# Two token parts under one weight load: a 512-column matmul in the last 64 key tiles, with GpSimd splits and one-hots in fours of tokens

## The chip, the cores and the metric

The kernel runs on one core of one Trainium2 chip. The metric is the device time of one execution in microseconds (us), lower is better. TensorE is written PE (its weight loads PEld), VectorE DVE, ScalarE ACT, GpSimd POOL, and SyncE SP.

## The reference

One residual block over 256 tokens of width 1024, in float32:

```
h = x + W_out( sig(g_conv) * ConformerConv(xn) + sig(g_attn) * DilatedAttn(xn) ),  xn = RMSNorm(x)
y = h + PEER(RMSNorm(h))

def peer(xn, w_q, sub_keys, u_tab, v_tab):          # 16384 experts of one neuron each
    q = (xn @ w_q)  ->  8 heads, 2 halves of 128
    s = q . sub_keys                                  # 128 scores per half
    top 16 of each half, top 16 of the 256 sums       -> 16 experts e and softmax gates per head
    h = einsum('thkd,td->thk', u_tab[e], xn)
    act = gelu(h) * gate
    y   = einsum('thk,thkd->td', act, v_tab[e])
```

## The kernel before, in words

**Stages.** A front part streams 76 weight tiles (projection, convolution, attention, output projection, queries). Then PEER is computed densely: 128 key tiles (rows of `u_tab`, each gives the activation of 128 experts for all 256 tokens), and 128 value tiles (rows of `v_tab`), which add up into the output. A tile is 128 x 1024 float32 and comes by one DMA of 512 KB into a ring `raw` of four slots.

**Two parts of a number.** Matmuls run on float32r operands. To keep float32 precision every weight tile is split: ACT rounds it into `hi` (`split_hi`, L310), and DVE or POOL subtracts into `lo` (`split_lo`, L323; `by_dve` says who: DVE takes slot 3, and from tile `G_SHARED` on slot 1 too, that is one tile in four before the 67th key tile and two in four after it). The normalised tokens stand as `nrm_hi` and `nrm_lo`, each 8 blocks of 256 columns. A key tile (`u_tile`, `product`, L1055) is 24 matmuls of 256 columns: for each of 8 blocks `hi` x `nrm_hi`, `hi` x `nrm_lo`, `lo` x `nrm_hi`, all summed in the left half of PSUM bank 4 or 5 (`bank[4 + j % 2][:, 0:T]`). ACT applies Gelu straight from the bank into `act` (`gelu`, L573), and PE may write a bank again when `gelu_done` says that the tile two before is through.

**The order of the tiles.** Tile n is computed while ACT splits tile n+3 (LEAD = 3): `split_hi` of tile n+3 waits until PE is through with tile n-1, whose slot it takes. In the first 64 key tiles DVE works at the same time on the selection of the experts (`top_step`: maxima and indices L857 to L862, candidate sums L871, table lookups L881, L886, L888 over 128 x 2048 elements), with its splits put between the steps in program order. At key tile 60 the selection is transposed on PE.

**The gates.** In the last 64 key tiles and the first 64 value tiles the gate values of all experts are made from one-hot rows: for each group of 8 tokens DVE writes `eqB`, `ohA`, `ohB` (`one_hots`, L965, L967, L971; float16, pairs of tokens innermost), PE does 16 small matmuls (`gates`, L1283), and DVE multiplies them into `act` (`multiply`, L983). There are 64 groups, one per two tiles. In `gate_body` (one turn is four tiles, j = 0 to 3) DVE does at even j a `multiply`, at odd j the `one_hots` of a later group, and then its split if it has one.

**Value tiles.** `v_tile` (L1326) has 12 matmuls of 512 columns. They use the activations split by ACT (L598, into slots of `nrm_hi`) and DVE (`low_part`, L990, into slots of `nrm_lo`). Two groups of one-hots for the second half of the gates are made by DVE before the first value tile.

Each engine takes its instructions in program order, and all waits are on semaphores.

Of the kernel before, what the change touches and what calls it, by code (L numbers as in the profile page):

```python
# [8 lines left out]
F32R = mybir.dt.float32r  # L9
# [6 lines left out]
P = 128  # L16
D = 1024
T = 256
# [34 lines left out]
TOK = 8  # L53
PAIR = 2
GROUPS_N = T // TOK
# [83 lines left out]

PAIRS = [(0, 2), (1, 3), (4, 6), (5, 7), (8, 10), (9, 11)]  # L140

# [10 lines left out]
def hybrid_block(nc, x_t, front, cols, rel_bias, onehot, sub_keys, u_tiles, v_tiles, out):  # L152
    toeplitz = nc.dram_tensor("toeplitz", (HEADS, P * BW), F32, kind="Internal").ap()
    with ExitStack() as ctx:
# [11 lines left out]
        lo = sb("lo", [P, RING, D], F32R)  # L166
        nrm_hi = sb("nrm_hi", [P, KB, T], F32R)
        nrm_lo = sb("nrm_lo", [P, KB, T], F32R)
        ident = sb("ident", [P, P])
# [35 lines left out]
        act = sb("act", [P, NK, T])  # L205
        iota_nk = sb("iota_nk", [P, NK, PAIR], F16)
        keys = sb("keys", [P, 2, T], F16)

        parts = sb("parts", [P, T // PAIR, 2, PAIR], F16)
        ohA = sb("ohA", [P, 2, TOK // PAIR, NK, PAIR], F16)  # L210
        eqB = sb("eqB", [P, 2, TOK // PAIR, HALF, PAIR], F16)
        ohB = sb("ohB", [P, 2, TOK // PAIR, 2, HALF, PAIR], F16)

# [54 lines left out]
        sc_ready = sem("sc_ready")  # L268
        gelu_done = sem("gelu_done")
        top_done, gexp, gate_ready, pick_T, pick_ready = [sem(s) for s in (  # L270
# [41 lines left out]
        def by_dve(base, j):  # L312

            return slot_of(base, j) == 3 or (base + j >= G_SHARED and slot_of(base, j) == 1)

# [67 lines left out]
        def _(pool):  # L383
# [20 lines left out]
            for g in range(N_FRONT + LEAD):  # L404
# [3 lines left out]
            pool.wait_ge(normed, 2 * KB)  # L408
            pool.iota(iota_nk[:, :, :], pattern=[[1, NK], [0, PAIR]], base=0, channel_multiplier=0,
                      allow_small_or_imprecise_dtypes=True).then_inc(const, 1)  # L410
# [7 lines left out]
        def _(a):  # L418
# [27 lines left out]
            def exp_of(s):  # L446
                c, pair = divmod(s, len(PAIRS))
                w = P * (c + 1)
                a.wait_ge(score_max, s + 1)
                for h in PAIRS[pair]:  # L450
# [138 lines left out]
            a.wait_ge(pick_ready, 2)  # L589
            with a.Fori(0, HALF // RING) as it:  # L590
                for j in range(RING):
                    split_hi(a, U0 + HALF + LEAD, it, j)
                    gelu(HALF, it, j)

# [26 lines left out]
        def _(dve):  # L621
# [79 lines left out]
            def score(s):  # L701

                c, pair = divmod(s, len(PAIRS))
                h0 = PAIRS[pair][0]
                w = P * (c + 1)
                job_done(dve, ("score", s))
                for r, h in enumerate(PAIRS[pair]):
# [237 lines left out]
            link(dve.tensor_scalar(pickf[:, 0, :], bank[7][:, 0:T], GATE_SCALE, None, ALU.mult))  # L945
            picked = pickf[:, 0, :].rearrange("p (a b) -> p a b", b=PAIR)
            link(dve.tensor_copy(parts[:, :, 0, :], picked))
# [4 lines left out]
            def one_hots(half, it, g):  # L952
# [3 lines left out]

                wait(dve, gate_mm, n - 1)

                def at(x, m):
                    return x.rearrange("p (a b) -> p a b", b=PAIR).unsqueeze(2).broadcast_to([P, TOK // PAIR, m, PAIR])  # L960

                def every_pair(x, m):
                    return x.unsqueeze(1).broadcast_to([P, TOK // PAIR, m, PAIR])

                dve.tensor_tensor(eqB[:, g % 2], every_pair(iota_nk[:, half * HALF:(half + 1) * HALF, :], HALF),  # L965
                                  at(keys[:, 1, t], HALF), ALU.is_equal).then_inc(second, 1)
# [3 lines left out]
                two = bass.ds(it * (2 * TOK // PAIR) + g * (TOK // PAIR), TOK // PAIR)  # L970
                dve.tensor_tensor(  # L971
                    ohB[:, g % 2].rearrange("p a i n b -> p (a i) n b"),
                    eqB[:, g % 2].unsqueeze(2).broadcast_to([P, TOK // PAIR, 2, HALF, PAIR]),
                    parts[:, two, :, :].rearrange("p a i b -> p (a i) b").unsqueeze(2)
                    .broadcast_to([P, 2 * TOK // PAIR, HALF, PAIR]), ALU.mult).then_inc(spread, 1)

# [9 lines left out]
            def low_part(base_i, it, j):  # L986
# [48 lines left out]
        def _(pe):  # L1035
# [106 lines left out]
            def scores(s):  # L1142
                c, pair = divmod(s, len(PAIRS))
                w = P * (c + 1)
                b = start(("score", s))
                freed(pe, ("kb", AB // 2 - 1))
                for r, h in enumerate(PAIRS[pair]):
                    rows = slice((h % 2) * HD, (h % 2 + 1) * HD)
# [122 lines left out]
            def u_tile(base_i, it, j):  # L1271
# [3 lines left out]
                ins.then_inc(pe_step, 1)  # L1275

            def gates(half, it, g):

                n = it * 2 + (half * GROUPS_N + g)
                pe.wait_ge(spread, n * 2 + 2)  # L1280
                for q in range(TOK):
                    for i in range(2):
                        ins = pe.matmul(bank[6 + g][:, q * HALF:(q + 1) * HALF], ohA[:, g, q // PAIR, :, q % PAIR],  # L1283
                                        ohB[:, g, q // PAIR, i, :, q % PAIR], start=i == 0, stop=i == 1, skip_group_check=True)
                ins.then_inc(gate_mm, 1)
# [133 lines left out]
```

## Time and profile before

| | |
|---|---|
| median of 3 runs | 1069.43 us (1066.47 to 1072.64) |
| the profiled execution's own time | 1069.04 us |
| its span, first to last instruction | 1067.3 us |
| mean granted PE clock | 0.988 of full speed |
| PE busy | 1049.8 us (98%) |
| DVE busy | 751.4 us (70%) |
| ACT busy | 509.7 us (48%) |
| POOL busy | 514.0 us (48%) |

The rows further down are of this execution. Times are us from the start of the span unless ns is written; L12 is line 12 of the kernel. Matmuls are pipelined, so the duration of one (280 ns for 256 columns) is longer than the distance from its start to the next one's, and it is the distance that counts.

### The profile page before, as it was taken

The numbers are of one execution on the slowest core, as the hardware profiler recorded it, in microseconds if no ns is written. First come the engines' busy times: TensorE is split into PE (matmuls) and PEld (weight loads), VectorE is DVE, ScalarE is ACT, GpSimd is POOL, SyncE is SP. The second block draws the span as 40 slices with busy tenths as digits, with TensorE's granted clock in tenths as the row PEclk, the third lists the DMA queues.
The fourth block names the chain that finished last, engine by engine and source line by source line (L and its number), as shares of the span: only waits on it lengthen the run. The fifth ranks groups of instructions, "written<-read, shape, count | busy, mean of one in ns | idle before, by whom it ended". The sixth has DMA issues, their size and how long they took to land.

```text
span 1067.3 us, 21882 instructions
## 1 busy us (share of the span) xinstructions
PE 1049.8 (98%) x7850; PEld 961.8 (90%) x7850; DVE 751.4 (70%) x1232; ACT 509.7 (48%) x798; POOL 514.0 (48%) x216
## 2 busy tenths in 40 slices
PE   8999999999999998999999999999999999999998
PEld 6999898999999998999999999978887777888886
DVE  5375868744079899918555555599999997777775
ACT  5453667545454443454444444444444444444553
POOL 3654452654646694964344333444434434444442
PEclk8999999999999998999999999999999999999999
DMA  5864342644535544465554455545554555666662
GB/s 195 267 209 139 125 149 84 216 160 141 182 133 183 191 148 166 140 214 174 167 172 158 161 173 168 166 158 177 177 172 162 177 177 178 197 196 188 190 194 97
DMA packets 52258, 181.91 MB, mean 170 GB/s; under 512 B 5851, under 2 KB 9051, under 8 KB 52092
## 3 DMA queue, kind: packets, MB, share of 16 engines
q1 hardware_dynamic: 52220, 181.41, 52.0%
q8 instruction: 24, 0.39, 0.1%
q14 instruction: 14, 0.11, 0.0%
HBM read 177.97 MB, written 3.41 MB: 170 GB/s over the span
## 4 chain that ended last, share of the span: by engine, by line
PE 91%; DVE 7%; issue 1%; ACT 1%; DMA 0%; SPq 0%; ACTq 0%; DVEq 0%
PE bank L1055 49%; PE bank L1326 33%; PE bank L1283 3%; PE bank L1136 2%; DVE lo L323 1%; PE bank L1065 1%; PE bank L1149 1%; PE bank L1263 1%; DVE gsig L829 1%; DVE prob L748 1%; DMA relx<-rel_bias 0%; DVE act L881 0%; DVE act L886 0%; DVE act L871 0%; PE bank L1243 0%
## 5 line engine op out<-in xcount | busy, mean ns | idle before, releaser
L323 POOL TENSOR_TENSOR lo<-raw,hi 128x1024 fp32r<-128x1024 f32 x202 | 511.1, 2535 | 538.5 <-ACT hi L310 538.1
L310 ACT CAST hi<-raw 128x1024 fp32r<-128x1024 f32 x332 | 347.9, 1048 | 200.9 <-PE bank L1326 189.8
L1055 PE MATMUL bank<-nrm_hi,hi 128*128 128x256 f32 x1504 | 433.4, 288 | 7.5 <-DVE lo L323 5.1
L1055 PE MATMUL bank<-nrm_lo,hi 128*128 128x256 f32 x1504 | 428.1, 285 | 0.0
L1055 PE MATMUL bank<-nrm_hi,lo 128*128 128x256 f32 x1504 | 427.9, 285 | 0.0
L1055 PEld LDWEIGHTS bank<-nrm_hi,hi 128*128 128x128 f32 x1504 | 291.1, 194 | 12.9 <-issue 7.7
L1055 PEld LDWEIGHTS bank<-nrm_lo,hi 128*128 128x128 f32 x1504 | 291.4, 194 | 0.1
L1055 PEld LDWEIGHTS bank<-nrm_hi,lo 128*128 128x128 f32 x1504 | 291.1, 194 | 0.0
L323 DVE TENSOR_TENSOR lo<-raw,hi 128x1024 fp32r<-128x1024 f32 x130 | 173.6, 1336 | 111.0 <-ACT hi L310 110.5
L990 DVE TENSOR_TENSOR nrm_lo<-act,nrm_hi 128x256 fp32r<-128x256 f32 x128 | 151.0, 1182 | 51.2 <-ACT nrm_hi L598 51.1
L1326 PE MATMUL bank<-hi,nrm_hi 128*128 128x512 f32 x512 | 160.6, 395 | 0.7 <-ACT nrm_hi L598 0.7
L1326 PE MATMUL bank<-hi,nrm_lo 128*128 128x512 f32 x512 | 158.9, 391 | 0.3 <-DVE nrm_lo L990 0.3
L1326 PE MATMUL bank<-lo,nrm_hi 128*128 128x512 f32 x512 | 158.0, 390 | 0.0
L573 ACT ACTIVATE act<-bank 128x256 f32 x128 | 49.1, 384 | 218.0 <-PE bank L1055 217.9
L1326 PEld LDWEIGHTS bank<-hi,nrm_lo 128*128 128x128 f32 x512 | 95.1, 188 | 22.9 <-DVE nrm_lo L990 3.7
L1326 PEld LDWEIGHTS bank<-lo,nrm_hi 128*128 128x128 f32 x512 | 96.1, 188 | 20.2
L1326 PEld LDWEIGHTS bank<-hi,nrm_hi 128*128 128x128 f32 x512 | 93.7, 188 | 18.7 <-issue 0.8
L983 DVE SCALAR_TENSOR_TENSOR act<-bank,act 128x512 f32 (+1 forms) x64 | 43.9, 685 | 83.6 <-PE bank L1283 83.6
L971 DVE TENSOR_TENSOR ohB<-eqB,parts 128x1024 f16<-128x1024 f16 x64 | 59.2, 925 | 0.0
L967 DVE TENSOR_TENSOR ohA<-iota_nk,keys 128x1024 f16<-128x1024 f16 x64 | 52.5, 820 | 0.0
L598 ACT CAST nrm_hi<-act 128x256 fp32r (+1 forms) x128 | 51.2, 402 | 0.1
L689 DVE SCALAR_TENSOR_TENSOR bank<-u_pad,prm,bank 128x256 f32<-128x256 f32 x116 | 46.7, 481 | 0.0
(172 smaller groups left out, 764.8 us busy)
## 6 DMA issues: line engine op xcount, KB each, us to landing
raw<-u_tiles SPq DMA_DIRECT2D x128, 512.0 KB, 3.4
raw<-v_tiles SPq DMA_DIRECT2D x128, 512.0 KB, 3.4
raw<-front SPq DMA_DIRECT2D x76, 512.0 KB, 3.4
toeplitz<-prob SPq DMA_DIRECT2D x12, 192.0 KB, 4.4
bias<-toeplitz SPq DMA_DIRECT2D x12, 128.0 KB, 4.1
resid<-x_t SPq DMA_DIRECT2D x2, 512.0 KB, 4.5
qk<-sub_keys SPq DMA_DIRECT2D x1, 1024.0 KB, 6.8
y<-act SPq DMA_DIRECT2D x2, 512.0 KB, 2.6
```

The source lines that it names most:

```text
L310: act_e.copy(hi[:, s, :], raw[:, s, :]).then_inc(hi_ready, 1)
L323: eng.tensor_tensor(lo[:, s, :], raw[:, s, :], hi[:, s, :].bitcast(F32), ALU.subtract)\
L573: a.activation(act[:, it * 4 + (base_i + j), :], bank[4 + j % 2][:, 0:T], ACT.Gelu).then_inc(gelu_done, 1)
L598: a.copy(nrm_hi[:, (base_i + j) % RING, :], act[:, it * 4 + (base_i + j), :]).then_inc(a_hi, 1)
L689: dve.scalar_tensor_tensor(out=acc[:, b, :] if w == TAPS - 1 else part_sum, in0=src, scalar=wt, in1=part_sum, op0=ALU.mult, op1=ALU.add).t ...
L967: dve.tensor_tensor(ohA[:, g % 2], every_pair(iota_nk[:, :, :], NK), at(keys[:, 0, t], NK), ALU.is_equal).then_inc(spread, 1)
L971: dve.tensor_tensor(ohB[:, g % 2].rearrange("p a i n b -> p (a i) n b"), eqB[:, g % 2].unsqueeze(2).broadcast_to([P, TOK // PAIR, 2, HALF, ...
L983: dve.scalar_tensor_tensor(out=av, in0=gv, scalar=1.0 / GATE_SCALE, in1=av, op0=ALU.mult, op1=ALU.mult)\
L990: dve.tensor_tensor(nrm_lo[:, s, :], act[:, it * 4 + (base_i + j), :], nrm_hi[:, s, :].bitcast(F32), ALU.subtract).then_inc(a_lo, 1)
L1055: ins = pe.matmul(dst, w_[:, s, u * P:(u + 1) * P], x_[:, k, :], start=first and i == 0 and p_ == 0, stop=last and i == n - 1 and p_ == 2)
L1283: ins = pe.matmul(bank[6 + g][:, q * HALF:(q + 1) * HALF], ohA[:, g, q // PAIR, :, q % PAIR], ohB[:, g, q // PAIR, i, :, q % PAIR], start= ...
L1326: ins = pe.matmul(bank[2 * c + half][:, :], a_[:, j, c * P:(c + 1) * P], v_[:, j, half * 512:(half + 1) * 512], start=False, stop=stop and ...
```

## The change

1. **Wide key tiles.** `nrm_hi` and `nrm_lo` become two interleaved views of one tensor `nrm`, so that the two parts of a block lie side by side in 512 columns. In the last 64 key tiles `u_tile` is replaced by `wide_tile`: per block one matmul of 512 columns (`hi` with both parts, into the whole bank) and one of 256 (`lo` with `nrm_hi`, into the left half): 16 matmuls instead of 24, for as many columns. The two halves of the bank are then added outside PE: ACT copies the right half to `half_sum` (`copy_cross`), DVE adds the left half to it (`add_halves`), ACT applies Gelu to the sum (`gelu_sum`, one tile later). PE may write a bank when `added` says that the tile two before is through.
2. **Order on ACT.** In these tiles ACT's order for tile n is: wait for the end of tile n, `copy_cross(n)`, `gelu_sum(n-1)`, `split_hi(n+3)`. Before it was `split_hi(n+3)`, which needs only the end of tile n-1, and then, at the end of tile n, `gelu(n)`.
3. **Order on DVE.** `add_halves(n)` stands behind the one-hots or the multiply of its turn and behind DVE's split of tile n+3.
4. **Splits.** From key tile 3 to key tile 66 `by_dve` says no: POOL does all splits there, DVE none. Afterwards they are shared as before.
5. **Fours.** The one-hots stand in fours of tokens instead of pairs (same number of elements and instructions; neighbouring rows of a matmul operand now lie 8 bytes apart instead of 4). `eqB` has one buffer instead of two, with a wait on DVE's own previous product.

```diff
-        nrm_hi = sb("nrm_hi", [P, KB, T], F32R)
-        nrm_lo = sb("nrm_lo", [P, KB, T], F32R)
+        nrm = sb("nrm", [P, KB, 2, T], F32R)
+        nrm_hi, nrm_lo = nrm[:, :, 0, :], nrm[:, :, 1, :]
...
-        ohA = sb("ohA", [P, 2, TOK // PAIR, NK, PAIR], F16)
-        eqB = sb("eqB", [P, 2, TOK // PAIR, HALF, PAIR], F16)
-        ohB = sb("ohB", [P, 2, TOK // PAIR, 2, HALF, PAIR], F16)
+        ohA = sb("ohA", [P, 2, TOK // QUAD, NK, QUAD], F16)
+        eqB = sb("eqB", [P, TOK // QUAD, HALF, QUAD], F16)
+        half_sum = sb("half_sum", [P, 2, T])
+        ohB = sb("ohB", [P, 2, TOK // QUAD, 2, HALF, QUAD], F16)
...
         def by_dve(base, j):
+            if U0 + LEAD <= base + j < G_SHARED:
+                return False
             return slot_of(base, j) == 3 or (base + j >= G_SHARED and slot_of(base, j) == 1)
...
             a.wait_ge(pick_ready, 2)
-            with a.Fori(0, HALF // RING) as it:
+            def copy_cross(it, j):
+                a.wait_ge(pe_step, it * 4 + (S_U + HALF + j + 1))
+                a.wait_ge(gelu_done, it * 4 + (HALF + j - 1))
+                a.copy(half_sum[:, j % 2, :], bank[4 + j % 2][:, T:2 * T]).then_inc(crossed, 1)
+            def gelu_sum(base, it, j):
+                a.wait_ge(added, it * 4 + (base + j + 1))
+                a.activation(act[:, it * 4 + (HALF + base + j), :], half_sum[:, (base + j) % 2, :], ACT.Gelu)\
+                 .then_inc(gelu_done, 1)
+            def key_round(it, first=False):
                 for j in range(RING):
+                    copy_cross(it, j)
+                    if not (first and j == 0):
+                        gelu_sum(-1, it, j)
                     split_hi(a, U0 + HALF + LEAD, it, j)
-                    gelu(HALF, it, j)
+            key_round(0, first=True)
+            with a.Fori(1, HALF // RING) as it:
+                key_round(it)
+            gelu_sum(HALF - 1, 0, 0)
...
             for i in range(HALF):
-                if by_dve(U0 + LEAD, i):
-                    split_lo(dve, U0 + LEAD, 0, i)
...
                 wait(dve, gate_mm, n - 1)
+                wait(dve, spread, n * 2)
...
+            def add_halves(it, j):
+                dve.wait_ge(crossed, it * 4 + (j + 1))
+                dve.tensor_tensor(half_sum[:, j % 2, :], bank[4 + j % 2][:, 0:T], half_sum[:, j % 2, :], ALU.add)\
+                   .then_inc(added, 1)
             def gate_body(half, it, first=False, last=False):
...
                     if by_dve(base + LEAD, j):
                         split_lo(dve, base + LEAD, it, j)
+                    if half == 0:
+                        add_halves(it, j)
...
+            def wide_tile(it, j):
+                b = bank[4 + j % 2]
+                if isinstance(it, int) and j < 2:
+                    pe.wait_ge(gelu_done, HALF + j - 1)
+                else:
+                    pe.wait_ge(added, it * 4 + (j - 1))
+                wait_lo(pe, U0 + HALF, it, j)
+                for k in range(KB):
+                    unit = slice(k * P, (k + 1) * P)
+                    pe.matmul(b[:, :], hi[:, j, unit], nrm[:, k, :, :].rearrange("p a t -> p (a t)"),
+                              start=k == 0, stop=False, skip_group_check=True)
+                    ins = pe.matmul(b[:, 0:T], lo[:, j, unit], nrm_hi[:, k, :],
+                                    start=False, stop=k == KB - 1, skip_group_check=True)
+                ins.then_inc(pe_step, 1)
             def u_and_gates(it):
                 for j in range(RING):
                     if j % 2 == 0:
                         gates(0, it, j // 2)
-                    u_tile(HALF, it, j)
+                    wide_tile(it, j)
```

## Rows read from the trace of the kernel before

**Rows 1.** The page: PE's share; the chain that ended last, by engine.

```profile
PE 1049.8 (98%) x7850; PEld 961.8 (90%) x7850; DVE 751.4 (70%) x1232; ACT 509.7 (48%) x798; POOL 514.0 (48%) x216
...
PE 91%; DVE 7%; issue 1%; ACT 1%; DMA 0%; SPq 0%; ACTq 0%; DVEq 0%
```

**Rows 2.** The chain in order of time: start, us, what.

```profile
415.26 63.39 PE bank L1055 x504
...
503.97 5.83 PE bank L1055 x48
509.80 0.50 PE bank L1283 x16
510.30 5.83 PE bank L1055 x48
...
687.44 5.84 PE bank L1055 x48
694.47 5.69 PE bank L1326 x24
...
889.98 173.48 PE bank L1326 x764
```

**Rows 3.** Who waited for whom, PE, key tiles 0 to 60: total, times, longest.

```profile
PE bank L1055 <- DVE lo L323: 5.1, 1, 5.1
```

**Rows 4.** Windows: length, busy PE, PEld, DVE, ACT, POOL, clock, DMA share, GB/s.

```profile
416.00:418.00 2.00, 2.00 (x12) 2.00 (x11) 2.00 (x11) 0.00 (x0) 0.00 (x0) 0.50 0.85 274
...
420.00:422.00 2.00, 2.00 (x14) 2.00 (x13) 2.00 (x9) 1.12 (x2) 0.00 (x0) 0.65 0.91 367
```

**Rows 5.** Timeline of ACT, two key tiles of the first half.

```profile
378.63 0.38 ACT L573 ACTIVATE act<-bank 128x256 f32 x1 [1.56 <-PE bank L1055]
...
381.51 0.39 ACT L573 ACTIVATE act<-bank 128x256 f32 x1 [1.42 <-PE bank L1055]
381.79 1.05 ACT L310 CAST hi<-raw 128x1024 fp32r<-128x1024 f32 x1
```

**Rows 6.** Timeline of all engines around the end of one late key tile.

```profile
566.46 0.28 PE L1055 MATMUL bank<-nrm_hi,lo 128*128 128x256 f32 x1
...
566.87 0.38 ACT L573 ACTIVATE act<-bank 128x256 f32 x1 [1.56 <-PE bank L1055]
...
567.25 1.05 ACT L310 CAST hi<-raw 128x1024 fp32r<-128x1024 f32 x1
...
568.34 1.23 DVE L323 TENSOR_TENSOR lo<-raw,hi 128x1024 fp32r<-128x1024 f32 x1 [0.27 <-ACT hi L310]
...
569.48 0.42 DVE L965 TENSOR_TENSOR eqB<-iota_nk,keys 128x512 f16<-128x512 f16 x1
...
570.42 0.68 DVE L971 TENSOR_TENSOR ohB<-eqB,parts 128x1024 f16<-128x1024 f16 x1
```

**Rows 7.** Instructions of one line: count, ns min/median/max, first and last start.

```profile
L826 DVE TENSOR_TENSOR gsig<-bank,gsig x8: 410/418/424, 196.5 to 216.9; 128x256 f32<-128x256 f32 x8
...
L479 ACT COPY gsig<-bank x16: 363/372/373, 114.9 to 169.8; 128x256 f32<-128x256 f32 x16
```

**Rows 8.** The same view for the POOL splits and the two-input lookups.

```profile
L323 POOL TENSOR_TENSOR lo<-raw,hi x202: 2337/2404/4472, 9.7 to 1051.0; 128x1024 fp32r<-128x1024 f32 x101
...
L881 DVE TENSOR_TENSOR act<-act,iota x4: 2293/3390/4492, 370.8 to 437.2; 128x2048 f32<-128x2048 f32 x4
...
L886 DVE TENSOR_TENSOR act<-act x4: 4381/4382/4384, 373.2 to 441.7; 128x2048 f32<-128x2048 f32 x4
```

**Rows 9.** Timelines of POOL and DVE during the selection.

```profile
385.79 11.05 POOL L323 TENSOR_TENSOR lo<-raw,hi 128x1024 fp32r<-128x1024 f32 x3 [0.26 <-ACT hi L310]
...
404.78 0.76 DVE L857 MAX8 act<-act 128x8 f32<-128x256 f32 x2
...
408.59 0.75 DVE L857 MAX8 act<-act 128x8 f32<-128x256 f32 x2
...
412.40 2.72 DVE L323 TENSOR_TENSOR lo<-raw,hi 128x1024 fp32r<-128x1024 f32 x1
```

**Rows 10.** Timeline of DVE and ACT at the change from keys to values.

```profile
692.05 0.69 DVE L971 TENSOR_TENSOR ohB<-eqB,parts 128x1024 f16<-128x1024 f16 x1
...
693.92 0.71 ACT L598 CAST nrm_hi<-act 128x256 fp32r<-128x256 f32 x2
```

More of the change, by code:

```diff
@@ L53 @@
 TOK = 8
-PAIR = 2
+QUAD = 4
 GROUPS_N = T // TOK
@@ L137 @@
     FREED[_job] = _n[freed_by_dve(_job)]
-PAIRS = [(0, 2), (1, 3), (4, 6), (5, 7), (8, 10), (9, 11)]
+QUADS = [(0, 2), (1, 3), (4, 6), (5, 7), (8, 10), (9, 11)]
 C_N1, C_N2, C_GLU, C_DW, C_DWB = 0, 8, 16, 24, 24 + CB * TAPS
@@ L205, in hybrid_block @@
         act = sb("act", [P, NK, T])
-        iota_nk = sb("iota_nk", [P, NK, PAIR], F16)
+        iota_nk = sb("iota_nk", [P, NK, QUAD], F16)
         keys = sb("keys", [P, 2, T], F16)
-        parts = sb("parts", [P, T // PAIR, 2, PAIR], F16)
-        ohA = sb("ohA", [P, 2, TOK // PAIR, NK, PAIR], F16)
-        eqB = sb("eqB", [P, 2, TOK // PAIR, HALF, PAIR], F16)
-        ohB = sb("ohB", [P, 2, TOK // PAIR, 2, HALF, PAIR], F16)
+        parts = sb("parts", [P, T // QUAD, 2, QUAD], F16)
+        ohA = sb("ohA", [P, 2, TOK // QUAD, NK, QUAD], F16)
+        eqB = sb("eqB", [P, TOK // QUAD, HALF, QUAD], F16)
+        half_sum = sb("half_sum", [P, 2, T])
+        ohB = sb("ohB", [P, 2, TOK // QUAD, 2, HALF, QUAD], F16)
         p3 = prob[:, :].rearrange("p (h n) -> p h n", n=BW)
@@ L268, in hybrid_block @@
         sc_ready = sem("sc_ready")
-        gelu_done = sem("gelu_done")
+        crossed, added, gelu_done = sem("crossed"), sem("added"), sem("gelu_done")
         top_done, gexp, gate_ready, pick_T, pick_ready = [sem(s) for s in (
@@ L408, in _ @@
             pool.wait_ge(normed, 2 * KB)
-            pool.iota(iota_nk[:, :, :], pattern=[[1, NK], [0, PAIR]], base=0, channel_multiplier=0,
+            pool.iota(iota_nk[:, :, :], pattern=[[1, NK], [0, QUAD]], base=0, channel_multiplier=0,
                       allow_small_or_imprecise_dtypes=True).then_inc(const, 1)
@@ L446, in exp_of @@
             def exp_of(s):
-                c, pair = divmod(s, len(PAIRS))
+                c, pair = divmod(s, len(QUADS))
                 w = P * (c + 1)
                 a.wait_ge(score_max, s + 1)
-                for h in PAIRS[pair]:
+                for h in QUADS[pair]:
                     pr = p3[:, h, c * P:c * P + w]
@@ L701, in score @@
             def score(s):
-                c, pair = divmod(s, len(PAIRS))
-                h0 = PAIRS[pair][0]
+                c, pair = divmod(s, len(QUADS))
+                h0 = QUADS[pair][0]
                 w = P * (c + 1)
                 job_done(dve, ("score", s))
-                for r, h in enumerate(PAIRS[pair]):
+                for r, h in enumerate(QUADS[pair]):
                     col = c * HEADS + h
@@ L945, in _ @@
             link(dve.tensor_scalar(pickf[:, 0, :], bank[7][:, 0:T], GATE_SCALE, None, ALU.mult))
-            picked = pickf[:, 0, :].rearrange("p (a b) -> p a b", b=PAIR)
+            picked = pickf[:, 0, :].rearrange("p (a b) -> p a b", b=QUAD)
             link(dve.tensor_copy(parts[:, :, 0, :], picked))
@@ L957, in one_hots @@
                 wait(dve, gate_mm, n - 1)
+                wait(dve, spread, n * 2)
                 def at(x, m):
-                    return x.rearrange("p (a b) -> p a b", b=PAIR).unsqueeze(2).broadcast_to([P, TOK // PAIR, m, PAIR])
+                    return x.rearrange("p (a b) -> p a b", b=QUAD).unsqueeze(2).broadcast_to([P, TOK // QUAD, m, QUAD])
                 def every_pair(x, m):
-                    return x.unsqueeze(1).broadcast_to([P, TOK // PAIR, m, PAIR])
-                dve.tensor_tensor(eqB[:, g % 2], every_pair(iota_nk[:, half * HALF:(half + 1) * HALF, :], HALF),
+                    return x.unsqueeze(1).broadcast_to([P, TOK // QUAD, m, QUAD])
+                dve.tensor_tensor(eqB[:, :, :, :], every_pair(iota_nk[:, half * HALF:(half + 1) * HALF, :], HALF),
                                   at(keys[:, 1, t], HALF), ALU.is_equal).then_inc(second, 1)
@@ L969, in one_hots @@
                 dve.wait_ge(second, n + 1)
-                two = bass.ds(it * (2 * TOK // PAIR) + g * (TOK // PAIR), TOK // PAIR)
+                two = bass.ds(it * (2 * TOK // QUAD) + g * (TOK // QUAD), TOK // QUAD)
                 dve.tensor_tensor(
                     ohB[:, g % 2].rearrange("p a i n b -> p (a i) n b"),
-                    eqB[:, g % 2].unsqueeze(2).broadcast_to([P, TOK // PAIR, 2, HALF, PAIR]),
+                    eqB[:, :, :, :].unsqueeze(2).broadcast_to([P, TOK // QUAD, 2, HALF, QUAD]),
                     parts[:, two, :, :].rearrange("p a i b -> p (a i) b").unsqueeze(2)
-                    .broadcast_to([P, 2 * TOK // PAIR, HALF, PAIR]), ALU.mult).then_inc(spread, 1)
+                    .broadcast_to([P, 2 * TOK // QUAD, HALF, QUAD]), ALU.mult).then_inc(spread, 1)
             def multiply(half, it, g):
@@ L1142, in scores @@
             def scores(s):
-                c, pair = divmod(s, len(PAIRS))
+                c, pair = divmod(s, len(QUADS))
                 w = P * (c + 1)
@@ L1146, in scores @@
                 freed(pe, ("kb", AB // 2 - 1))
-                for r, h in enumerate(PAIRS[pair]):
+                for r, h in enumerate(QUADS[pair]):
                     rows = slice((h % 2) * HD, (h % 2 + 1) * HD)
@@ L1282, in gates @@
                     for i in range(2):
-                        ins = pe.matmul(bank[6 + g][:, q * HALF:(q + 1) * HALF], ohA[:, g, q // PAIR, :, q % PAIR],
-                                        ohB[:, g, q // PAIR, i, :, q % PAIR], start=i == 0, stop=i == 1, skip_group_check=True)
+                        ins = pe.matmul(bank[6 + g][:, q * HALF:(q + 1) * HALF], ohA[:, g, q // QUAD, :, q % QUAD],
+                                        ohB[:, g, q // QUAD, i, :, q % QUAD], start=i == 0, stop=i == 1, skip_group_check=True)
                 ins.then_inc(gate_mm, 1)
```

## The prediction

> **What bounds the kernel now.** I read the page first: the reader is to see that PE is busy in 98% of the span and carries 91% of the chain that ended last [rows 1]. So the time is, to first order, the number of matmuls times their distance, plus the few places where PE is kept waiting. The chain in order of time gives the distances [rows 2]. In the late key part two tiles and one group of gates take 510.30 - 503.97 = 6.33 us. A key tile alone, from the timeline of ACT, takes 381.51 - 378.63 = 2.88 us [rows 5], or 120 ns for each of 24 matmuls; a group of gates with the restart behind it is then 6.33 - 5.76 = 0.57. Sixty-four value tiles of 12 matmuls took 173.48 us, or 226 ns for 512 columns [rows 2]. Two matmuls of 256 are 240, so joining two saves 14 ns.
>
> The list of waits shows one real stall of PE before the gates: 5.1 us for a DVE split [rows 3]. DVE reached that split late, at 412.40, because selection steps stand ahead of it in its queue [rows 9], and PE resumed at 415.26 [rows 2]. The windows show what came after: clock 0.50 at 416 to 418, and a mean of 0.65 at 420 to 422, so about 1.4 of these 2 us at the lower level (1.2 GHz) [rows 4]. From 415.26 to 421.4 that is 6.1 us at half speed, about 2.8 us lost beyond the stall (rounded down for its edges). The stall cost 7.9 us in all.
>
> **Splits to POOL, first half.** DVE's splits leave, so the stall of 5.1 and its clock, together 7.9, go. What takes its place? A POOL split takes 2.40 [rows 8] for a tile of 2.88: with all four tiles it fits with 0.48 to spare. But an operation of DVE with two SBUF inputs and a POOL split exclude each other: the lookup L881 takes 2.29 undisturbed and 4.49 disturbed, L886 4.38 each time [rows 8], and three POOL splits beside them needed 11.05 instead of 7.2 [rows 9]. Each such lookup holds POOL back by 2.29. The slack: POOL's split of tile n+3 ends after the end of tile n-1 by 0.29 (PE to ACT: the last matmul starts at 566.46, the next would at 566.58, ACT starts at 566.87 [rows 6]), 0.28 for Gelu [rows 5], 1.05 for the rounding and 0.04 to the next engine [rows 6], and 2.40, in all 4.06; it is needed after three tiles, 8.64. That leaves 4.6. First burst, four lookups and the candidate sum behind them: 5 x 2.29 = 11.5, less 0.48 in each of some 8 tiles (3.8), less 4.6: PE waits 3.1. Between the bursts lie four pairs of candidate maxima, 408.59 - 404.78 = 3.8 us each [rows 9], 15 us or 5.4 tiles, which give back 2.6. Second burst: 4 x 2.29 = 9.2, less 3.4, less 2.6: 3.2. I take **+6.3**; bounds +2 (DVE waits for POOL more often than it holds it) and +10. Small waits spread over a dozen tiles should leave the clock up. The selection itself loses its pacing and ends earlier; nothing waits for it before key tile 52. Where the one-hots begin, DVE comes some 2 us earlier and meets a fuller POOL: 0, at most +2.
>
> **Wide tiles.** A tile becomes 8 x (226 + 120) = 2.77 us, 0.11 less; if nothing waits, 64 tiles give **-7.0**. The Trainium skill speaks against so much: TensorE: Matmul & The Clock Gate, section "Back-to-back issue gap", gives an isolated gap of N/2.4 plus 2.5 ns, by which joining saves only 2.5 ns, 1.3 us over 512 joins. The rows have 120 ns where that rule has 109, and decide here.
>
> **The new wait.** PE may start tile n+2 only when `added` is up for tile n. For even n, DVE's split of tile n+3 stands ahead of the addition, and that split waits for ACT's rounding, which now stands behind the copy and a Gelu. From the end of tile n: 0.29 to ACT; copy 0.38 (a copy of this size takes 0.37 [rows 7], and it has two waits; ACT's step at 566.87 was 0.38 long [rows 6], the shorter one 0.28 [rows 5]); Gelu of tile n-1 0.28; rounding 1.05; 0.04 to DVE; split 1.14 (568.34 to 569.48 [rows 6]); addition 0.42 (a PSUM operand and an SBUF operand of this size [rows 7]); 0.14 until PE starts again (412.40 + 2.72 = 415.12 [rows 9] to 415.26 [rows 2]). That makes 3.74. What covers it is tile n+1 and a group of gates: 2.77 + 0.57 = 3.34. So PE waits 0.40 at every second tile, and a pair takes 3.74 + 2.77 = 6.51 instead of 6.33: +0.18, times 32 pairs **+5.8**, the saving of the wide tiles already in it. The bounds: both short ACT steps at 0.28, the addition 0.33, the restart 0.04: 3.45, a pair 6.22, -3.5 in all. Or both ACT steps 0.38, 0.10 for register values of the double waits (an estimate, from the 0.1 between ACT's two kinds of step), and 512 columns at 231 ns (694.47's 5.69 and its neighbours over 24 matmuls [rows 2]): 6.76, +13.8. For odd n the one-hots stand ahead of the addition, 1.62 (569.48 to the end of 570.42's [rows 6]), but they don't wait for tile n: `added` comes some 2.9 after its end, before the 3.34. POOL's splits fall between the one-hots and the next split of DVE, so I see no collision there. DMAs keep their number, and a slot is freed early enough.
>
> **From keys to values.** Before, both groups of one-hots for the second half were ready (692.05 + 0.69) before the last key tile ended (687.44 + 5.84 = 693.28) [rows 2, 10], and PE went on at 694.47 after a group of gates. Now they stand in DVE's queue behind the addition of the last tile: that ends at 0.29 + 0.38 + 0.04 + 0.42 = 1.13 after the tile; two groups 3.2; one of their steps is caught behind a POOL split (2.4, ACT's rounding ends at 2.0, just then); the low part of the first value tile 0.4: 7.1 us. Eight of its matmuls are still to come (1.8) and the second tile (2.7): 11.6 after the end. Before it was 694.47 + 5.69 - 693.28 = 6.9. So **+4.8**; bounds +2.5 (no collision) and +8 (the idle stretch drops the clock, as in rows 4).
>
> **Fours.** Same elements and counts on DVE: 0. On PE the operands of the gates are read 8 bytes apart instead of 4. No row shows such a read; the nearest is the group at 0.50 for 16 [rows 2]. I take 0, the upper bound is twice the time, 64 x 0.5 = +32, the lower -2 (gates cheaper by a sixteenth: nothing shows more). Closest to the unchanged row, because only the stride changes. The Trainium skill, SBUF - State Buffer, section "Door 1: The DMA port swizzle", wants two hits in a 16-byte line; 8 bytes just meet that. No run here has shown it.
>
> The second wait in `one_hots` is on work long done: 0, covered by DVE's idle time.
>
> **Sum** against the profiled execution's own 1069.04: -7.9 + 6.3 + 5.8 + 4.8 + 0 = +9.0, or 1078. The median of the runs, 1069.43, is 0.4 from it, so 1078 serves for both.
>
> **Rivals.**
> - *The late addition is covered, POOL keeps up.* The chain of 3.74 has to shrink below 3.34 in effect; break-even is at 3.56, which its lower bound of 3.45 passes. For it: every piece is near its bound. Against: the order on ACT and DVE is fixed. Then -7.9 + 2 - 7.0 + 2.5: 1059. Chance 0.20.
> - *POOL becomes the bound.* If a lookup keeps winning against POOL (L886 alternates with it each time), the lag of a burst exceeds 6 us, PE waits 15 instead of 6, and its clock may fall: 1087 to 1092. For it: rows 8 and 9. Against: POOL is free during the maxima. Chance 0.13.
> - *Strided operands slow the gates.* 1078 + 32 x 1, less if part is hidden: about 1105. Chance 0.07.
> - *Joining saves next to nothing*, 2.5 ns a join as a mechanism of issue: the wide tile is 2.86, a pair 3.74 + 2.86 = 6.60: 1081. Against: 226 ns for 512 columns. Chance 0.03. The page that has this gap is the one named above.
> - The forecast holds the rest, 0.57, with its own range 1066 to 1090.
>
> **How the numbers follow.** About 0.5% (5.3 us) is what a measurement of this kernel tells from no change: 1064.1 to 1074.8 count as the same. Faster: 0.17, nearly all of the first rival. Same: 0.20 (0.15 low end of the forecast, 0.03 of the first rival, 0.02 of the second). Slower: 0.63. The range 1061 to 1096 leaves out about half of the first rival's cases and the third rival.
>
> **What would show each step.** The list of waits: PE for DVE's addition, some 32 times 0.3 to 0.5 us, at tiles after gates. The chain: pairs of late key tiles 6.4 to 6.7 apart; 6.11 would make the first rival right. Matmuls of 512 columns 226 ns apart in the wide tiles. No clock dip at 416, PE waits for POOL splits between 370 and 450 adding up to 6. A gap of some 3 to 5 us before the first value tiles. A group of gates still 0.50. The prediction is wrong if additions come within 3.3 us of a tile's end, or if POOL never falls behind.

## The result, and the profile after

The changed kernel takes 1093.56 us, the median of 6 runs (1092.19 to 1096.96), against 1068.41 for the kernel before (6 runs, 1066.47 to 1072.64). The ratio is 1.0235, 95% interval 1.0207 to 1.0264: slower by 25 us. The forecast was slower by 9. The profiled execution took 1092.22, its span is 1090.3 us, 23.0 more than the span before.

The page, against [rows 1]:

```profile
PE 1072.1 (98%) x7338; PEld 960.9 (88%) x7338; DVE 752.3 (69%) x1280; ACT 530.8 (49%) x862; POOL 547.1 (50%) x232
...
PE 88%; DVE 4%; issue 4%; POOL 3%; ACT 1%; DMA 0%; SPq 0%; POOLq 0%; ACTq 0%; DVEq 0%
```

PE has 512 matmuls fewer and is busy 22 us longer. PE is still in 98% of the span, so something that PE does has become longer; it is not waiting more. The chain in order of time (start, us, what) answers to [rows 2]:

```profile
473.74 11.50 PE bank L1084 x96
485.24 1.00 PE bank L1328 x16
...
505.36 1.01 PE bank L1328 x16
...
512.07 1.01 PE bank L1328 x16
...
518.68 1.00 PE bank L1328 x16
...
704.58 4.83 PE bank L1371 x20
709.41 1.01 PE bank L1328 x16
...
716.96 5.52 PE bank L1371 x24
722.48 1.01 PE bank L1328 x16
...
913.04 173.49 PE bank L1371 x764
```

The reader is to see the group of gates: L1328 is `gates` with its 16 small matmuls, and it takes 1.01 us where it took 0.50 [rows 2]. All 64 groups are like that, in the key part and in the value part. Two key tiles and a group are 518.68 - 512.07 = 6.61 apart (some 6.71, as 512.07 - 505.36; why, no run shows); they were 6.33. The tail after the gates is the same 173.49 us. The view of one line (ns min/median/max, first and last start) tells the same of the single instruction; before, the matmul's median was 193 ns and the weight load's 97:

```profile
L1328 PEld LDWEIGHTS bank<-ohB,ohA x1024: 112/118/140, 485.1 to 906.0; 128*128 128x128 f16 x171
L1328 PE MATMUL bank<-ohB,ohA x1024: 227/243/248, 485.1 to 906.0; 128*128 128x64 f16 x171
```

Who waited for whom on PE, in all and longest, against [rows 3]:

```profile
PE bank L1084 <- POOL lo L326: 3.2, 4, 1.3
PE bank L1328 <- DVE ohB L992: 2.5, 1, 2.5
PE bank L1371 <- DVE nrm L1011: 2.3, 2, 1.9
```

The wait of 5.1 for a DVE split is gone, and small waits for POOL's splits stand in its place. No row says that PE waited for DVE's addition.

Where the 23.0 us of the span are, stage by stage, from the chains of both kernels (the end of the changed kernel's last key tile, 698.0, from its timeline):

| stage | before | after | difference | forecast |
|---|---|---|---|---|
| up to the first key tile | 297.8 | 296.1 | -1.7 | 0 |
| first 64 key tiles | 193.0 | 189.1 | -3.9 | -1.6 |
| last 64 key tiles, 32 groups | 202.5 | 212.8 | +10.3 | +5.8 |
| end of the keys to the end of the second value tile | 6.9 | 11.4 | +4.5 | +4.8 |
| the value tiles with gates, 31 groups | 189.8 | 203.6 | +13.8 | 0 |
| the rest | 173.5 | 173.5 | 0 | 0 |

The first row is how one execution differs from another. The last but one is the surprise: in that part only the fours change anything (the single `eqB` buffer costs nothing there: the change in pairs, further down, has it too and takes 189.8). 31 x 0.51 is 15.8, of which 2.0 are missing. Some 1.0 of them are small delays that the longer groups cover: a pair with its group is 6.53, and before it was 6.05, but 6.15 from about 821 on. Most of the rest is that the 24 matmuls between two groups take 5.52 where they took 5.55.

### The profile page after: what moved, and what is told of

Read it like the earlier page. It is cut to its first block, busy times and chain, and to the rows that moved or that the text cites. A ratio compares the mean times of both kernels' runs of the same rounds, so it can differ in the third digit from the quotient of the medians.

```text
span 1090.3 us, 21138 instructions
## 1 busy us (share of the span) xinstructions
PE 1072.1 (98%) x7338; PEld 960.9 (88%) x7338; DVE 752.3 (69%) x1280; ACT 530.8 (49%) x862; POOL 547.1 (50%) x232
## 4 chain that ended last, share of the span: by engine, by line
PE 88%; DVE 4%; issue 4%; POOL 3%; ACT 1%; DMA 0%; SPq 0%; POOLq 0%; ACTq 0%; DVEq 0%
PE bank L1371 32%; PE bank L1084 28%; PE bank L1316 11%; PE bank L1328 6%; PE bank L1318 5%; POOL lo L326 3%; PE bank L1165 2%; PE bank L1094 1%; PE bank L1178 1%; PE bank L1292 1%; DVE gsig L851 1%; DVE prob L770 1%; DMA relx<-rel_bias 0%; DVE lo L326 0%; PE bank L1272 0%
## 5 line engine op out<-in xcount | busy, mean ns | idle before, releaser
L1084 PE MATMUL bank<-nrm,hi 128*128 128x256 f32 x1984 | 363.5, 286 | 5.4 <-POOL lo L326 3.2
L1084 PEld LDWEIGHTS bank<-nrm,hi 128*128 128x128 f32 x1984 | 311.9, 193 | 11.3 <-issue 3.4
L1371 PE MATMUL bank<-hi,nrm 128*128 128x512 f32 x1024 | 282.2, 392 | 2.3 <-DVE nrm L1011 2.3
L1084 PE MATMUL bank<-nrm,lo 128*128 128x256 f32 x992 | 282.1, 284 | 0.0
L1371 PEld LDWEIGHTS bank<-hi,nrm 128*128 128x128 f32 x1024 | 190.3, 189 | 41.0 <-DVE nrm L1011 3.1
L1011 DVE TENSOR_TENSOR nrm<-act,nrm 128x256 fp32r<-128x256 f32 x128 | 168.7, 1320 | 66.5 <-ACT nrm L620 66.5
L1084 PEld LDWEIGHTS bank<-nrm,lo 128*128 128x128 f32 x992 | 191.8, 193 | 0.0
L1316 PE MATMUL bank<-nrm,hi 128*128 128x512 f32 x512 | 183.0, 400 | 0.0
L1371 PE MATMUL bank<-lo,nrm 128*128 128x512 f32 x512 | 158.1, 390 | 0.0
L1318 PE MATMUL bank<-nrm,lo 128*128 128x256 f32 x512 | 142.8, 279 | 0.0
L1316 PEld LDWEIGHTS bank<-nrm,hi 128*128 128x128 f32 x512 | 96.7, 189 | 21.3
L1371 PEld LDWEIGHTS bank<-lo,nrm 128*128 128x128 f32 x512 | 96.1, 188 | 20.2
L1318 PEld LDWEIGHTS bank<-nrm,lo 128*128 128x128 f32 x512 | 96.5, 189 | 0.0
L1328 PEld LDWEIGHTS bank<-ohB,ohA 128*128 128x128 f16 x1024 | 63.0, 118 | 16.0 <-issue 13.1
L1328 PE MATMUL bank<-ohB,ohA 128*128 128x64 f16 x1024 | 74.5, 242 | 2.5 <-DVE ohB L992 2.5
```

Source lines behind the costliest of these rows:

```text
L1011: dve.tensor_tensor(nrm_lo[:, s, :], act[:, it * 4 + (base_i + j), :], nrm_hi[:, s, :].bitcast(F32), ALU.subtract).then_inc(a_lo, 1)
L1084: ins = pe.matmul(dst, w_[:, s, u * P:(u + 1) * P], x_[:, k, :], start=first and i == 0 and p_ == 0, stop=last and i == n - 1 and p_ == 2)
L1316: pe.matmul(b[:, :], hi[:, j, unit], nrm[:, k, :, :].rearrange("p a t -> p (a t)"), start=k == 0, stop=False, skip_group_check=True)
L1318: ins = pe.matmul(b[:, 0:T], lo[:, j, unit], nrm_hi[:, k, :], start=False, stop=k == KB - 1, skip_group_check=True)
L1371: ins = pe.matmul(bank[2 * c + half][:, :], a_[:, j, c * P:(c + 1) * P], v_[:, j, half * 512:(half + 1) * 512], start=False, stop=stop and ...
```

## Experiments: the stride of the gates' operands

Two theories of the stride stood against each other. R: a read takes time by the bytes that its stride spans, so 4 bytes apart costs already something, 8 doubles it and 16 doubles it again. E: up to 4 bytes the stride is free, and beyond it every element costs the same, wherever the next one is, so that 16 bytes cost no more than 8. Against both stood what the prediction had taken, that the gates by themselves are as fast in fours; then their 1.01 would come from what stands around them in the changed kernel.

**Fours alone** (the kernel before with one constant changed).

```diff
-PAIR = 2
+PAIR = 4
```

> The kernel before with one edit: one-hots in fours of tokens instead of pairs, so PE reads both gate operands 8 bytes apart instead of 4. Theory S (the strided reads are the cause that the prediction gave a chance of 0.07): in the trace of the changed kernel a group of gates takes 1.01 us instead of 0.50, 64 groups are 32.6 us, so this kernel takes 1068.4 + 32.6 = 1101. Rival W (the groups are slow because of what stands around them in the changed kernel: the wide matmuls, the interleaved token parts, the waits): groups stay at 0.50 and the time is 1068.

Measured: 1098.71 us against 1070.02, ratio 1.0273 (1.0245 to 1.0301). Its chain:

```profile
505.48 1.01 PE bank L1283 x16
506.49 5.80 PE bank L1055 x48
512.28 1.01 PE bank L1283 x16
513.29 5.80 PE bank L1055 x48
```

One constant costs more than the whole change. The groups are slow with nothing else changed: 64 x 0.51 = 32.6 on PE. A pair with its group grows by less, from 6.33 to 512.28 - 505.48 = 6.80, because the 48 matmuls beside it take 5.80 where they took 5.83; the small delays of the value part are covered again, and 28.7 arrive in the median.

**Which operand?** `ohA` is the operand loaded as weights, `ohB` the one that moves through the array. In these two kernels the widths are apart: `QA` for `ohA`, `QB` for `eqB`, `ohB` and `parts` (the lines in which DVE writes them follow suit and are left out here).

```diff
-PAIR = 2
+PAIR = 4
+QA, QB = 4, 2        # weights_fours; moving_fours has QA, QB = 2, 4
...
-                        ins = pe.matmul(bank[6 + g][:, q * HALF:(q + 1) * HALF], ohA[:, g, q // PAIR, :, q % PAIR],
-                                        ohB[:, g, q // PAIR, i, :, q % PAIR], start=i == 0, stop=i == 1, skip_group_check=True)
+                        ins = pe.matmul(bank[6 + g][:, q * HALF:(q + 1) * HALF], ohA[:, g, q // QA, :, q % QA],
+                                        ohB[:, g, q // QB, i, :, q % QB], start=i == 0, stop=i == 1, skip_group_check=True)
```

> The kernel before, only ohA (the operand loaded as weights of the gate matmuls) in fours, ohB (the moving one) in pairs. A group has 16 loads of 128 columns and 16 matmuls of 64. If the load's stride costs: the group goes towards 1.0 us and the time to 1101; if only the moving operand's stride costs: 0.50 and 1068. The load row of the changed kernel went from 97 to 118 ns and the matmul row from 193 to 243, which fits either.

> The kernel before, only ohB (the moving operand of the gate matmuls) in fours, ohA in pairs. The complement of the run before: 1101 if the moving operand's stride costs all, 1068 if the weights' does; if each costs its own part, the two runs lie between and add up to 33 us.

Measured: weights in fours 1073.16 (ratio 1.0037, 1.0019 to 1.0055), moving operand in fours 1097.38 (1.0269, 1.0239 to 1.0299), both against 1070.02. The chain of the first, then of the second:

```profile
503.86 0.55 PE bank L1284 x16
504.41 5.83 PE bank L1056 x48
```

```profile
502.74 0.98 PE bank L1284 x16
503.72 5.79 PE bank L1056 x48
```

So of the 0.51 that a group became longer, the moving operand alone brings 0.48; the weights alone bring 0.05, or 3.1 us in the median.

**Eights, and no stride at all.** The first is `PAIR = 8` in the kernel before, neighbours 16 bytes apart. The second leaves the writing in pairs as it is, but PE reads runs of neighbouring elements; what it leaves out is the right choice of elements, so its gate values are not the reference's and only its time counts:

```diff
-                        ins = pe.matmul(bank[6 + g][:, q * HALF:(q + 1) * HALF], ohA[:, g, q // PAIR, :, q % PAIR],
-                                        ohB[:, g, q // PAIR, i, :, q % PAIR], start=i == 0, stop=i == 1, skip_group_check=True)
+                        ins = pe.matmul(bank[6 + g][:, q * HALF:(q + 1) * HALF], ohA[:, g].rearrange("p a n b -> p (a n b)")[:, q * NK:(q + 1) * NK],
+                                        ohB[:, g].rearrange("p a i n b -> p (a i n b)")[:, (2 * q + i) * HALF:(2 * q + i + 1) * HALF], start=i == 0, stop=i == 1, skip_group_check=True)
```

> The kernel before with one-hots in eights: PE reads both gate operands 16 bytes apart. Pairs (4 bytes) have 0.50 us a group, fours (8 bytes) 1.01. Theory R (the moving operand costs by the bytes that its stride spans): another doubling, 2.0 us a group, 64 x 1.0 more than fours: some 1163. Rival E (beyond 4 bytes every element costs one access, wherever the next one is): the group stays near 1.0 and the time near 1099.

> The kernel before, DVE's one-hots unchanged in pairs, but PE reads 128 and 64 neighbouring elements (2 bytes apart) of the same buffers for each gate matmul; this leaves out the right choice of rows, so the gate values are not the reference's. Theory R: the stride of 4 bytes costs already, and a group falls below 0.50 towards 0.25, 64 x 0.25 = 16 us less: 1054. Rival E, and the count of columns (64 at 120 ns per 256 would be 30 ns, 16 of them 0.48): the group stays at 0.50 and the time at 1069.

Measured: eights 1158.79 against 1069.36 (ratio 1.0839, 1.0812 to 1.0867); dense reads 1069.93 (0.9992, 0.9975 to 1.0009). The chain of eights, then of dense reads:

```profile
503.77 1.99 PE bank L1283 x16
505.76 5.75 PE bank L1055 x48
```

```profile
503.40 0.48 PE bank L1283 x16
503.88 5.83 PE bank L1055 x48
```

A group takes 0.48 at a stride of 2 bytes, 0.50 at 4, 1.01 at 8, 1.99 at 16, with both operands at that stride. From 8 to 16 it doubles: that refutes E, and R's 1163 was near. From 2 to 4 it does not, which refutes R's lower half, by which dense reads would have brought 1054: pairs are all but free. So neither theory holds over the whole range. Up to 4 bytes one matmul with its load takes 30 to 31 ns, which is what 64 columns would take at the key tiles' 120 ns for 256 (an estimate across two types); at 8 bytes it takes 63, at 16 bytes 124. What in the memory makes it so no run shows. Only these four points were measured, all in float16, and for 16 bytes the two operands were not parted.

The Trainium skill, SBUF — State Buffer, section "Door 1: The DMA port swizzle", says that two accesses in each 16-byte line are enough for full bandwidth, and that in bf16 one can stride up to 8 elements for free. These runs disagree for TensorE's moving operand: 8 bytes apart cost twice the time (0.98 against 0.50 for a group), and 16 bytes, with the weights so too, four times. By the skill the fours would have cost nothing here, which is also the value that the prediction took; the measurement decides.

## Experiments: what is left of the change without the fours

**The change in pairs.** A theory, L in the expectation: the late addition that was forecast is there, and the slow gates hide it. The rival: the addition comes in time in any case.

```diff
-QUAD = 4
+QUAD = 2
```

> The changed kernel with one edit: fours back to pairs; wide tiles, POOL splits and the order of the waits stay. If S holds, a group of gates is 0.50 again. Then two theories differ on what is left. Theory L (late addition, as in the prediction): in the trace of the changed kernel the addition of an even tile ended 3.51 after the tile's end and PE restarts some 0.14 later, 3.65, while cover is only 2.78 + 0.55 = 3.33: pairs of late key tiles take 3.65 + 2.78 = 6.43, PE waits 0.3 at each, and the time is 1093.6 - 32.6 + 32 x 0.33 = 1071.5. Rival C (covered): pairs take 6.11 and the time is 1061. Rival W: groups stay at 1.0 and the time near 1093.

Measured: 1074.04 against 1070.02, ratio 1.0049 (1.0031 to 1.0066), 19.5 less than the change with fours. A group takes 0.50 again. PE's list of waits has a new row, and the chain shows the rest of the stall as issue around the addition, once in every pair:

```profile
PE bank L1316 <- DVE half_sum L1017: 1.3, 7, 0.2
```

```profile
485.33 0.50 PE bank L1328 x16
...
517.18 0.43 DVE half_sum L1017
...
523.00 0.61 issue
523.61 0.43 DVE half_sum L1017
...
530.12 0.43 DVE half_sum L1017
```

The timeline (start, us, then the instruction, and in brackets the idle time before it with its releaser) has two restarts of PE for a tile after the gates:

```profile
562.54 0.42 DVE L1017 TENSOR_TENSOR half_sum<-bank,half_sum 128x256 f32<-128x256 f32 x1
...
563.10 0.49 PE L1316 MATMUL bank<-nrm,hi 128*128 128x512 f32 x1 [0.19 <-DVE half_sum L1017]
...
569.52 0.50 PE L1316 MATMUL bank<-nrm,hi 128*128 128x512 f32 x1
...
691.82 0.28 PE L1318 MATMUL bank<-nrm,lo 128*128 128x256 f32 x1
```

This pair takes 569.52 - 563.10 = 6.42; the additions above are 6.43 and 6.51 apart. From the first group (485.33) to the end of the last key tile (691.82 + 0.28 = 692.10) it is 206.8 us, or 6.46 for a pair. Without a wait a pair takes 6.13, as the first two do here and all do in the next experiment; so 0.33 are lost in each on average. With groups of 1.01 there is nothing left to lose: 6.13 + 0.51 = 6.64 is more than the 6.46 that the wait makes of a pair, and the changed kernel shows 6.61, or 6.65 on average (212.8 / 32). That is why the fours cost 28.7 us in the median by themselves and 19.5 here: they hid the wait for the addition, some 10 us. In the last 64 key tiles they cost 212.8 - 206.8 = 6.0 here, and 32 x 0.48 = 15.4 in the kernel before. The timeline of the changed kernel, from the end of one key tile (568.81, where the next one's first matmul stands):

```profile
568.81 0.39 PE L1316 MATMUL bank<-nrm,hi 128*128 128x512 f32 x1
...
569.08 0.37 ACT L597 COPY half_sum<-bank 128x256 f32<-128x256 f32 x1 [1.91 <-PE bank L1318]
...
569.35 0.42 ACT L602 ACTIVATE act<-half_sum 128x256 f32 x1
...
569.67 1.04 ACT L311 CAST hi<-raw 128x1024 fp32r<-128x1024 f32 x1
...
570.74 1.23 DVE L326 TENSOR_TENSOR lo<-raw,hi 128x1024 fp32r<-128x1024 f32 x1 [2.58 <-ACT hi L311]
...
571.58 1.17 PE L1328 MATMUL bank<-ohB,ohA 128*128 128x64 f16 x16
...
571.88 0.42 DVE L1017 TENSOR_TENSOR half_sum<-bank,half_sum 128x256 f32<-128x256 f32 x1
...
572.56 0.47 PE L1316 MATMUL bank<-nrm,hi 128*128 128x512 f32 x1
```

Copy, Gelu, rounding, DVE's split, and then the addition, which ends at 572.30, 3.49 after the tile; with the 0.14 of a restart 3.63. PE is busy until about 572.6 with the wide tile (571.58 - 568.81 = 2.77) and the gates (1.01), and starts the next one without a wait.

**The addition ahead of DVE's split,** in the same kernel:

```diff
+                    if half == 0:
+                        add_halves(it, j)
                     if by_dve(base + LEAD, j):
                         split_lo(dve, base + LEAD, it, j)
-                    if half == 0:
-                        add_halves(it, j)
```

> The changed kernel with pairs (1074.0) and one more edit: DVE does the addition of a tile before its split of a later tile, instead of behind it. Theory L: the addition of an even tile ends 0.29 + 0.38 + 0.04 + 0.42 = 1.13 after the tile instead of 3.5, under the cover of 3.3; pairs of late key tiles fall from 6.43 to 6.11, 32 x 0.32 = 10 us: 1064. Rival (the wait for the addition isn't what spaces the tiles; the wide matmuls with the restart behind the gates are): pairs stay at 6.43, 1074. The splits come 0.34 later, with 5 us to spare.

Measured: 1061.95 against 1069.36, ratio 0.993 (0.9912 to 0.9949). The chain:

```profile
515.72 0.50 PE bank L1328 x16
...
521.85 0.50 PE bank L1328 x16
...
527.99 0.50 PE bank L1328 x16
```

A pair is 6.13, and PE waits for no addition any more. The last 64 key tiles take 196.3 us where they took 206.8: 10.5 less. The spans of the profiled executions (1072.6 and 1059.8) are 12.8 apart; of the other 2.3, 2.0 are a clock that fell in the first and not in the second (last section). Each median against that of the kernel before beside it, +4.0 and -7.4, gives 11.4. So the wait was a matter of two instructions' order on DVE, not of joining the matmuls.

**GpSimd's splits alone,** in the kernel before:

```diff
         def by_dve(base, j):
+            if U0 + LEAD <= base + j < G_SHARED:
+                return False
```

> The kernel before with only by_dve changed: POOL does all splits of key tiles 3 to 66. Two parts of the prediction are at stake: the stall of 5.1 with its clock, 7.9 in all, goes, and PE waits for POOL instead. The changed kernel's trace has 3.2 us of such waits and restarts, and its first 64 key tiles took 189.1 us against 193.0. Theory: 1070 - 4 = 1066, the same net as there. Rival (the forecast's own +6.3 of waits): 1068.4. Rival (the 5.1 and its clock were particular to one profiled run): no gain, or a loss, 1070 to 1073.

Measured: 1065.15 against 1069.36, ratio 0.9959 (0.9942 to 0.9976). The waits and two windows (length, busy PE, PEld, DVE, ACT, POOL, clock, DMA share, GB/s), against [rows 3, 4]:

```profile
PE bank L1057 <- POOL lo L325: 3.1, 4, 1.3
```

```profile
416.00:418.00 2.00, 2.00 (x19) 2.00 (x18) 2.00 (x1) 0.60 (x1) 2.00 (x2) 1.00 0.58 211
...
370.00:450.00 80.00, 76.86 (x635) 76.16 (x635) 57.13 (x80) 36.07 (x54) 78.64 (x28) 1.00 0.55 180
```

The stall and its half clock are gone, and the first 64 key tiles take 189.1 us instead of 193.0, as in the changed kernel; with four waits of at most 1.3 the granted clock stays at 1.00. POOL is busy in 78.64 of 80 us: it is nearly the bound, but it is not.

**The change from keys to values.** Two attempts to take its 4.5 us back, both on top of the kernel with the addition first. The theories said 1058 and 1059; by the rivals there was nothing to gain, 1061 to 1062. In the first DVE makes both groups of one-hots for the second half in the last turn of the key loop, in the second one of them there and the other behind the first value tile's low part.

```diff
+                    elif half == 0:
+                        one_hots(1, 0, j // 2)
...
-                one_hots(half, 0, 0)
-                one_hots(half, 0, 1)
+                if half == 0:
+                    one_hots(half, 0, 0)
+                    one_hots(half, 0, 1)
```

> The kernel of the run with pairs and the addition first (1062.0), and one more edit: the two groups of one-hots for the second half are made in the last turn of the first half, in the two places where that turn makes none, instead of after the last addition. Theory T (the change from keys to values costs because these one-hots stand behind the last addition): there the second value tile ended 11.4 after the last key tile, before 6.9; this comes back to some 7.0 plus 0.8 for copy and addition ahead of the last Gelu, 3.7 less: 1058.3. Rival (the value tiles wait for the later Gelu, the low part and POOL's exclusion, whatever the place of the one-hots): 1061 to 1062.

Measured: 1062.74 against 1069.05, ratio 0.9939 (0.9917 to 0.9961). The waits and the windows (columns as above):

```profile
PE bank L1374 <- ACT nrm L620: 2.5, 1, 2.5
```

```profile
686.00:688.00 2.00, 0.30 (x1) 0.33 (x2) 1.22 (x3) 1.61 (x5) 1.48 (x1) 0.82 0.95 217
688.00:690.00 2.00, 2.00 (x6) 1.49 (x6) 2.00 (x3) 1.11 (x2) 0.89 (x1) 0.50 0.11 45
```

The second of the two early groups stood ahead of the last addition, which ended at 686.8 for a tile that ended at 684.7. So ACT's first value split came late, PE idled for 2.5 us, and the clock fell to its lower level (1.2 GHz) behind it: 24 value matmuls took 7.11 instead of 5.55. The second value tile ended 10.1 after the last key tile, against 11.4 in the kernel with the addition first. The second attempt, as edited from the first:

```diff
-                    elif half == 0:
-                        one_hots(1, 0, j // 2)
+                    elif half == 0 and j == 1:
+                        one_hots(1, 0, 0)
...
                     one_hots(half, 0, 0)
-                    one_hots(half, 0, 1)
-                if half == 1:
+                else:
                     low_part(0, 0, 0)
+                one_hots(half, 0, 1)
```

> Pairs and the addition first, and of the two groups of one-hots for the second half only the first is made early (in the last turn, beside key tile 125), the second behind the last addition and the low part of the first value tile, so that neither stands ahead of the last addition. In the run with both early, the second value tile ended 10.1 after the last key tile (PE waited 2.5 for ACT's rounding, which waited for the last addition, and the clock then fell to 0.50 for a moment). Theory Q (what matters is DVE's queue ahead of the last addition and of the low part): addition at 1.13, Gelu, rounding and low part by 2.6, matmuls until 3.5 + 4.5: the second value tile ends 8 to 9 after the key tile, 2.5 to 3.4 less than with both late: 1059. Rival (POOL's exclusion of the second group delays the next low part as much): no gain, 1062.

Measured: 1061.28 against 1069.37, ratio 0.9921 (0.9897 to 0.9944). The waits:

```profile
PE bank L1374 <- ACT nrm L620: 2.0, 1, 2.0
...
PE bank L1374 <- DVE nrm L1011: 1.2, 2, 0.9
```

The one long wait became two shorter ones, the low part on DVE took 2.1 instead of 0.4 beside a POOL split, and the clock stood at 0.50 from 686 to 688 all the same. The second value tile ended 10.7 after the last key tile. Neither attempt can be told from the kernel with the addition first (1061.95), so this stage was not won, as the rivals had it. That kernel and the last one are the best of the study, 0.7 and 0.8% below the kernel before.

## Why the prediction was wrong, step by step

**Fours: this step failed.** "I take 0 ... Closest to the unchanged row, because only the stride changes." Measured by itself: a group goes from 0.50 to 1.01, +32.6 on PE, +28.7 in the median; in the changed kernel +19.5 of its 25. The bound of twice the time was on paper, and it was exact, but it stood there as rival with a chance of 0.07. The mistake is in how the value was chosen: no row showed such a read, and then an unchanged price was called the nearest row. That rival's own figure of 1105 was too high by 11: it took off 5 for what is hidden, where the prediction's own numbers already had more (the whole 0.40 of each late addition, since 2.77 + 1.07 is over 3.74: 12.8, which makes 1097).

**Luck.** "Slower" came true mainly through the step that failed. And that 1093.56 lies inside the stated range of 1061 to 1096 is luck: the range was drawn to leave this rival out, and the time falls below its end only because the fours hide the late addition and the other terms came out lower in sum.

**The new wait: right, a little too dear.** Forecast 3.74 after the tile's end, measured 3.63 (in the changed kernel, with the restart as forecast); a pair 6.51, measured 6.46 on average in pairs. The term was +5.8; the last 64 key tiles took 206.8 - 202.5 = +4.3. Its cause, the split ahead of the addition, is shown: exchanging the two took the pair to 6.13. The first rival had this as 6.11. Its 1059 took the full -7.0, though, for which the addition has to be there within 3.34, and the prediction's own lower bound of 3.45 gives -3.5; only another order reaches it.

**Wide tiles: right.** 2.77 forecast and measured. The rival by which a join saves 2.5 ns would have made the tile 2.86. It is refuted.

**Splits to POOL: right in kind, too dear.** The stall and the clock's fall behind it went. PE's waits for POOL are 3.2 where 6.3 were forecast. The first 64 key tiles came out at -3.9 instead of -1.6, so the stall with its clock was worth some 7.1 and not 7.9 (193.0 - 189.1 + 3.2, an estimate). That every lookup holds POOL back by the full 2.29 gave twice the wait that was measured; how the two engines share was not tested by itself. The rival that POOL becomes the bound is refuted.

**From keys to values: right.** +4.8 forecast; +4.5 measured in the changed kernel and in the one with the addition first, +6.5 in the profiled execution of the change in pairs, where the clock fell as well.

**The sum without the failed step:** 1078 forecast, 1074.04 measured for the change in pairs. Its span is 1072.6 - 1067.3 = 5.3 longer where +9.0 was forecast: -1.5 up to the first key tile (one execution against another), -3.9 in the first 64 key tiles instead of -1.6, +4.3 in the last 64 instead of +5.8, +6.5 from keys to values instead of +4.8, and nothing behind. So the sign of this change, taken without its fours, was right too, if only just: 1.0049.

## What to carry to other kernels

Count a matmul's stride as a cost of its own: keep neighbouring elements of a 2-byte moving operand at most 4 bytes apart, and put a wider stride on the operand that is loaded as weights, if one has to have it (8 bytes there cost 0.05 us a group against 0.48). Where no row shows an operation in the new form, "it stays as it is" is a guess like its upper bound, and dear ones deserve their bound in the forecast. When a step is added to a queue that another engine waits on, put what is waited for ahead of what merely has to be done: here that order alone was worth some 11 us, and turned a small loss into a gain.

## What the runs showed of the hardware

- 16 float16 matmuls of 64 columns take 0.48, 0.50, 1.01 and 1.99 us with both operands at a stride of 2, 4, 8 and 16 bytes. A stride of 8 bytes in the moving operand alone takes 0.98, in the weights alone 0.55.
- DVE writes the one-hots in pairs, fours or eights in the same time (`ohB` 684, 685 and 685 ns), and does not tell of the cost that PE has with them.
- An idle stretch of PE of the same length may be followed by either clock. In the change in pairs PE idled 2.5 and 2.4 us around a group of gates, and the clock stood at 0.50 from 698 to 702; in the kernel with the addition first it idled 2.5 and 2.4 us at the same place, and the clock stayed at 1.00:

```profile
700.00:702.00 2.00, 2.00 (x6) 1.52 (x6) 2.00 (x5) 0.00 (x0) 0.00 (x0) 0.50 0.11 20
```

```profile
688.00:690.00 2.00, 2.00 (x9) 1.68 (x10) 2.00 (x4) 0.00 (x0) 0.00 (x0) 1.00 0.40 158
```

What decides between the two is open; the difference is some 2 us of one execution (24 value matmuls and a group end 13.4 instead of 11.4 after the last key tile).
